# Gate columns and the last 120 mz columns in one block of weights, in a fused attention and mLSTM kernel

## The reference, cut to what matters

```
h = rms_norm(x, pre_norm_g)
proj = h @ w_in          # 1024 x 4616: aq ak av az mq mk mv mo mz (512 columns each), mi (4), mf (4)
ya = moba_attention(rope(aq), rope(ak), av);  ya = rms_norm(ya) * silu(az)
q, k = silu(causal_conv(mq | mk))
hm = mlstm(q, k, mv, mi + i_bias, mf + f_bias)      # 4 heads of 128
ym = sigmoid(mo) * groupnorm(hm) * silu(mz)
out = x + rms_norm((ya | ym) @ w_out) * post_g
```

## Time and profile before

| | us |
|---|---|
| median of 3 runs (lowest, highest) | 319.71 (317.78, 320.05) |
| the profiled execution's own time | 318.38 |
| its span, first to last instruction | 316.6 |
| PE busy | 308.4 (97%) |
| DVE busy | 225.9 (71%) |
| ACT busy | 164.9 (52%) |
| POOL busy | 96.7 (31%) |

### The profile page before, as it was taken

How to read it: one execution, slowest core, us unless ns; L and a number is a source line. 1 busy time by engine, 2 the same in 40 slices (tenths; PEclk the granted TensorE clock), 3 DMA queues, 4 the chain that set the end, 5 groups by cost and what they waited for, 6 DMA issues and landing times.

```text
span 316.6 us, 4991 instructions
## 1 busy us (share of the span) xinstructions
PE 308.4 (97%) x1595; PEld 255.7 (81%) x1595; DVE 225.9 (71%) x509; ACT 164.9 (52%) x337; POOL 96.7 (31%) x121
## 2 busy tenths in 40 slices
PE   7999999999999999999999999999999999999992
PEld 4888888878888888888888888778888888888882
DVE  3544999748998699968998568965577766856534
ACT  3448856287345324573147573385556976453201
POOL 3701006066450114002220026592711984000000
PEclk9999999999999999999999999999999999999998
DMA  7941553956725486654865433211220474310111
GB/s 233 313 99 36 158 144 94 164 154 155 142 69 135 135 151 204 182 144 114 181 193 183 114 77 88 71 66 34 67 68 0 127 185 157 134 68 0 66 68 67
DMA packets 29177, 38.30 MB, mean 121 GB/s; under 512 B 3672, under 2 KB 15296, under 8 KB 29152
## 3 DMA queue, kind: packets, MB, share of 16 engines
q1 hardware_dynamic: 27424, 34.51, 36.7%
q0 software_dynamic: 1568, 3.34, 7.3%
q10 hardware_dynamic: 160, 0.14, 0.1%
HBM read 33.68 MB, written 4.29 MB: 120 GB/s over the span
## 4 chain that ended last, share of the span: by engine, by line
PE 82%; DVE 7%; issue 4%; DMA 3%; ACT 2%; DVEq 0%; POOLq 0%; POOL 0%; SPq 0%; ACTq 0%
PE bank L1501 21%; PE bank L1503 21%; PE bank L1502 20%; PE bank L1553 4%; PE bank L1849 3%; PE bank L1793 3%; DMA w_raw<-in_w_in 3%; PE bank L1814 3%; PE bank L1646 2%; DVE w_lo L1061 2%; DVE farena L1173 1%; PE bank L1743 1%; PE bank L1534 1%; PE bank L1804 1%; PE bank L1647 1%
## 5 line engine op out<-in xcount | busy, mean ns | idle before, releaser
L788 ACT ACTIVATE w_hi<-w_raw 128x512 fp32r<-128x512 f32 x71 | 43.7, 626 | 63.1 <-PE bank L1503 50.8
L1501 PE MATMUL bank<-w_hi,xT_hi 128*128 128x512 f32 (+1 forms) x180 | 72.5, 403 | 0.0
L1503 PE MATMUL bank<-w_hi,xT_lo 128*128 128x512 f32 (+1 forms) x180 | 69.7, 387 | 0.0
L1502 PE MATMUL bank<-w_lo,xT_hi 128*128 128x512 f32 (+1 forms) x180 | 69.4, 385 | 0.0
L1061 DVE TENSOR_TENSOR w_lo<-w_raw,w_hi 128x512 fp32r<-128x512 f32 x64 | 45.6, 724 | 10.3 <-ACT w_hi L788 10.2
L1501 PE MATMUL bank<-xT_hi,w_hi 128*128 128x512 f32 x128 | 50.8, 397 | 0.0
L1503 PE MATMUL bank<-xT_hi,w_lo 128*128 128x512 f32 x128 | 50.1, 392 | 0.0
L1502 PE MATMUL bank<-xT_lo,w_hi 128*128 128x512 f32 x128 | 50.0, 390 | 0.0
L1503 PEld LDWEIGHTS bank<-w_hi,xT_lo 128*128 128x128 f32 x180 | 33.8, 188 | 7.1
L1501 PEld LDWEIGHTS bank<-w_hi,xT_hi 128*128 128x128 f32 x180 | 33.9, 188 | 5.9 <-issue 0.4
L1502 PEld LDWEIGHTS bank<-w_lo,xT_hi 128*128 128x128 f32 x180 | 34.0, 189 | 5.5
(11 more groups left out here) (215 smaller groups left out, 583.4 us busy)
## 6 DMA issues: line engine op xcount, KB each, us to landing
w_raw<-in_w_in SPq DMA_DIRECT2D x72, 256.0 KB, 3.0
w_raw<-in_w_out SPq DMA_DIRECT2D x16, 256.0 KB, 2.9
kq_rows<-stage SPq DMA_DIRECT2D x8, 256.0 KB
gy<-kq_rows SPq DMA_DIRECT2D x8, 256.0 KB, 3.5
gy<-in_x SPq DMA_DIRECT2D x4, 512.0 KB, 5.9
out_y<-gy SPq DMA_DIRECT2D x7, 256.0 KB, 2.0
farena<-in_x SPq DMA_DIRECT2D x4, 256.0 KB, 4.3
farena<-in_x SPq DMA_DIRECT2D x2, 512.0 KB, 6.3
```

The costliest lines, as they stand in the source:

```text
L788: a.activation(hi, raw, ACT.Copy).then_inc(w_hi_done, 1)
L1501: pe.matmul(o, hi, m_hi, start=start, stop=False)
L1502: pe.matmul(o, hi, m_lo, start=False, stop=False)
L1503: return pe.matmul(o, lo, m_hi, start=False, stop=stop)
```

## The change

The 8 gate columns and the last 120 columns of mz (`MIX_W`) make one block of 128 weight columns, loaded like the mq and mk blocks in two "heads" slots, 7 and 8, ahead of mv's last slot (now 9). `mix_slot` multiplies it with the weights stationary: 24 matmuls of 512 columns into bank 7, rows 0 to 119 mz, 120 to 127 gates. `gate_rows_of`, `wg`, its DMA, its clearing and its four DVE instructions go. DVE scales bank 7 (`scaled_rows`), and two stream shuffles repeat the gate rows; ACT copies the unscaled block into `mix_rows`. The mz slots (now 58 to 65) take 392 columns (`MZ_W`), and four transposes (`mz_mixed`) put the 120 columns behind them into each bank. `mix_rows` is the tile of `causal`, so POOL builds the mask later, behind the first mz slot. All slot numbers from mq on are higher by 2. On ACT the first sum of squares moves ahead of cut 6, the mix copy, Abs and Exp come ahead of `mv_high`, and the i gate's bias stays behind it; two more cuts come ahead of it, and so on DVE ahead of `mv_low`.

```diff
+MIX_W = P - 8
+MZ_W = AW - MIX_W
+MIX = MG - MIX_W
+SLOTS = [("in", "cols", k, MVC) for k in range(NK - 1)]
+SLOTS += [("in", "heads", k, MIX) for k in (0, 4)] + [("in", "cols", NK - 1, MVC)]
+def width(n):
+    return MZ_W if S_MZ <= n < S_MZ + NK else AW
...
-            g.memset(wg[:].bitcast(F32), 0.0).then_inc(wg_clear, 1)
-            g.memset(causal[:], 0.0).then_inc(cleared, 1)
...
+            g.wait_ge(w_used, S_MZ + 1)
+            g.memset(causal[:], 0.0).then_inc(cleared, 1)
+            g.wait_ge(cleared, 5)
+            g.affine_select(out=causal[:, SEQ - P:], in_=causal[:, SEQ - P:], compare_op=ALU.is_ge, fill=FAR, base=0,
+                            pattern=[[-1, P]], channel_multiplier=1).then_inc(causal_done, 1)
...
-                if k >= 6:
-                    x_squares(k - 6)
-            x_squares(2)
-            x_squares(3)
-            for n in range(RING, RING + 4):
+                if k >= 5:
+                    x_squares(k - 5)
+            cut(RING)
+            x_squares(NT - 1)
+            for n in range(RING + 1, RING + 6):
                 cut(n)
-            a.wait_ge(gate_ps, 1)
-            a.wait_ge(gate_clear, 1)
-            a.activation(gate_low_rows, bank[7][P // 2:, :], ACT.Copy).then_inc(gate_split, 1)
+            a.wait_ge(scaled, 1)
+            a.activation(mix_rows[:], bank[7][:], ACT.Copy).then_inc(mix_done, 1)
+            a.wait_ge(gate_sb, 1)
+            a.activation(rows[0], f_rows[96:112, :], ACT.Abs, bias=bcol[:, 1:2]).then_inc(absf_done, 1)
+            a.wait_ge(absf_done, 1)
+            a.activation(rows[1], rows[0], ACT.Exp, scale=-1.0).then_inc(expf_done, 1)
             for t in range(NT):
                 mv_high(t)
...
-            link(v.tensor_tensor(gate_rows, bank[7][0:P // 2, :], gate_low_rows, ALU.add))
-            v.tensor_tensor(gate_rows, gate_rows, rbc[0:P // 2, :], ALU.mult).then_inc(gate_sb, 1)
             cut(RING + 2)
-            cut(RING + 3)
+            v.wait_ge(w_used, S_MIX + 2)
+            v.tensor_tensor(scaled_rows, bank[7][:], rbc[:], ALU.mult).then_inc(scaled, 1)
+            v.wait_ge(scaled, 1)
+            v.stream_shuffle(f_rows, scaled_rows, [28 + i % MH for i in range(32)]).then_inc(gate_sb, 1)
+            v.stream_shuffle(i_rows, scaled_rows, [24 + i % MH for i in range(32)]).then_inc(gate_sb, 1)
+            for n in range(RING + 3, RING + 6):
+                cut(n)
             for t in range(NT):
                 mv_low(t)
...
+            def mix_slot(c):
+                low_done(pe, S_MIX + c)
+                pe.wait_ge(xt_lo, x_parts(4 * c + 3))
+                for kk in range(4):
+                    k = 4 * c + kk
+                    mm = product(bank[7][:], *w_part(S_MIX + c, slice(kk * P, (kk + 1) * P)), xT_hi[:, k, :],
+                                 xT_lo[:, k, :], k == 0, k == NK - 1)
+                mm.then_inc(w_used, 1)
...
-            gate_rows_of()
+            mix_slot(0)
             rx_rows()
+            mix_slot(1)
             mv_slot(NK - 1)
...
+            def mz_mixed(t):
+                pe.wait_ge(v_raw, t + 1)
+                pe.transpose(bank[t][:, MZ_W:], mix_rows[0:MIX_W, t * P:(t + 1) * P], ident[0:MIX_W, 0:MIX_W])
```

More of the change, by code:

```diff
@@ L318, in build @@
         rows = [gy[0:16, i // 4, i % 4, :] for i in range(8)]
-        gate_rows, gate_low_rows = (stage[0:P // 2, i, :] for i in range(2))
+        gate_rows = stage[0:P // 2, 0, :]
+        mix_rows = causal
+        scaled_rows, i_rows, f_rows = (stage[:, i, :] for i in range(1, NT))
         bcol = pcol[0:16, R_BIAS:R_END]
@@ L550, in _ @@
                 if kind == "cols":
-                    src = w[0, k * P:(k + 1) * P, c:c + AW]
-                    dst = w_raw[:, n % RAW, :]
+                    src = w[0, k * P:(k + 1) * P, c:c + width(n)]
+                    dst = w_raw[:, n % RAW, 0:width(n)]
                 else:
@@ L614, in _ @@
             g.memset(upad[:, :, 0:KCONV - 1], 0.0).then_inc(cleared, 1)
-            g.wait_ge(cleared, 5)
+            g.wait_ge(cleared, 4)
             g.memset(mhalf[:], -0.5).then_inc(consts, 1)
             g.wait_ge(ident_done, 1)
-            g.affine_select(out=causal[:, SEQ - P:], in_=causal[:, SEQ - P:], compare_op=ALU.is_ge, fill=FAR, base=0,
-                            pattern=[[-1, P]], channel_multiplier=1).then_inc(consts, 1)
             g.affine_select(out=causalT[:], in_=causalT[:], compare_op=ALU.is_ge, fill=FAR, base=0,
@@ L784, in cut @@
                     a.wait_ge(w_used, n - RING + 1)
-                hi, raw = w_hi[:, n % RING, :], w_raw[:, n % RAW, :]
+                hi, raw = w_hi[:, n % RING, 0:width(n)], w_raw[:, n % RAW, 0:width(n)]
                 if by_blocks(n):
@@ L824, in _ @@
                 x_hi(k)
-                if k >= 6:
-                    x_squares(k - 6)
-            x_squares(2)
-            x_squares(3)
-            for n in range(RING, RING + 4):
-                cut(n)
-            a.wait_ge(gate_ps, 1)
-            a.wait_ge(gate_clear, 1)
-            a.activation(gate_low_rows, bank[7][P // 2:, :], ACT.Copy).then_inc(gate_split, 1)
+                if k >= 5:
[3 more added lines that the diff above has]
+            for n in range(RING + 1, RING + 6):
+                cut(n)
+            a.wait_ge(scaled, 1)
[4 more added lines that the diff above has]
+            a.activation(rows[1], rows[0], ACT.Exp, scale=-1.0).then_inc(expf_done, 1)
             for t in range(NT):
                 mv_high(t)
[L837 to L841, removed]
+            a.wait_ge(gate_sb, 2)
+            a.activation(rows[6], i_rows[96:112, :], ACT.Identity, bias=bcol[:, 0:1]).then_inc(igate_done, 1)
             def decays(h, j):
@@ L1057, in cut @@
                 v.wait_ge(w_hi_done, n + 1)
-                lo, raw, hi = w_lo[:, n % RING, :], w_raw[:, n % RAW, :], f32(w_hi[:, n % RING, :])
+                cols = slice(0, width(n))
+                lo, raw, hi = w_lo[:, n % RING, cols], w_raw[:, n % RAW, cols], f32(w_hi[:, n % RING, cols])
                 if by_blocks(n):
@@ L1128, in gate_low @@
                 v.wait_ge(gate_sb, 1)
-                link(v.tensor_scalar(rows[3], gate_rows[32:48, :], bcol[:, 1:2], 0.0, ALU.add, ALU.min))
+                link(v.tensor_scalar(rows[3], f_rows[96:112, :], bcol[:, 1:2], 0.0, ALU.add, ALU.min))
                 v.wait_ge(expf_done, 1)
@@ L1373, in mask @@
                     v.wait_ge(prob_done, s - 1)
+                if s == 0:
+                    v.wait_ge(causal_done, 1)
                 at = score_at(s)
@@ L1542, in by_slot @@
                         free(t)
-                    mm = product(bank[t][:], *part(k, t), *w_part(n), k == 0, k == nk - 1)
+                    mm = product(bank[t][:, 0:width(n)], *part(k, t), *w_part(n, slice(0, width(n))), k == 0,
+                                 k == nk - 1)
                     if k == nk - 1 and t < NT - 1:
```

39 lines of the change are left out of this document (16 added, 23 removed).

## The result

The changed kernel is slightly slower: median 321.5 us (19 runs) against 318.13 us for the kernel before (19 runs, the first three among them). Its four longest runs (323.4 to 323.6 us) count as slow and are left out of the ratio, which compares the means of the others, 320.74 us, and of the kernel before, 318.53 us: 1.0069, 95% interval 1.0043 to 1.0095, which is +2.2 us (+1.4 to +3.0). By the medians it is +3.4 us. The forecast was 320.6 us within 317.1 to 323.0, +0.8 us.

The account below looks back on a forecast made before the run. PE's unbroken stream was taken as the bound, other engines hidden only while they stay ahead. +1.7 (mix for gate products) +0.7 (gate chain) -1.6 (kept of mz) = +0.8 us on median 319.71: 320.5, stated as 320.6, range 317.1 to 323.0.

Parts of the forecast that it names:

- PE's own sum: PE's matmuls: +1.7 us for mix slots replacing gate products, -4.5 for narrow mz slots, +0.4 for transposes: -2.4 us.
- The first half as a whole: Mix path in place of the gate products, up to `weighted`: +1.7 us on PE and +0.7 from the later gate work.
- The waits of the start: PE's `rx_rows` waiting for POOL's `rx`: `rx` comes about 0.6 us earlier, at 30.8, so costed at nothing.
- The gate chain: DVE's run from mix slot 1 through `gate_low` to the first decay masks: without room, so PE loses +0.7 us.
- The mz stage: PE needs 4.1 us less up to `z_part(0, 0)` but waits for DVE's `mz_gate`, keeping only 1.6 us.
- the shift is carried to the end: Behind `z_part(0, 0)` PE is again behind DVE by more than a microsecond, so the shift there stays.
- The first, PE bounds the mz stage: Rival: DVE's run shortens with PE, the whole 4.1 us is kept, gate chain without loss: 317.3 us, chance 0.2.
- The second, a gate chain 3 us late: Rival: gate work misses its slot loads, 3 us late instead of 0.7 at the first decay masks: 322.9 us, chance 0.15.
- The third, 392 columns at the price of 512: Rival: mz matmuls of 392 columns still step by 0.227 us, so mz gives +0.4: 322.5 us, chance 0.05.

Follow-up runs that it names:

- the control: The kernel before with the same three waits that hold back POOL's cuts of mo slots, nothing else changed: ratio 1.0000, median 317.96 us.

## Why the prediction was right, and what it missed

**PE's own sum** held. `rx_rows` began at 31.20, forecast 31.26. The narrow matmuls step by 0.177 us (taken: 0.180), and the four transposes add 0.47 us (taken: 0.44). The first half as a whole: +2.4 us forecast, +2.5 between the profiled executions at `weighted`, +2.4 by the ratio of the kernel with full mz slots.

**The waits of the start** cost nothing, as costed: `rx` was done at 30.5 us (forecast 30.8, before 31.36), ahead of `rx_rows` at 31.20. The earlier sum of squares is the reason given; no kernel was run without it.

**The gate chain.** `gate_low` was forecast for 43.4 us and came at 43.12; the wait for `weighted` for 1.4 us and was 1.5. That the wait follows the start of `gate_low` is likely, not shown. The two kernels with the chain shorter on ACT have waits of 0.8 and 0.6 us, less than any other with the mix path. But in those others `gate_low` starts 11.9 us behind `rx_rows` every time, and the wait is anything from 0.9 to 1.5 us. So the 1.5 us of the profile agree with the forecast of 1.4 in part by luck. The reason, too, was half wrong. The step said that DVE carries the chain; up to `gate_low` ACT does, by its mix copy, Abs, Exp, `mv_high` and the i gate, and two DVE cuts taken out of the way changed nothing. The prediction's own times had ACT at 41.0 us ahead of DVE's last three cuts; only its reading of them named DVE.

**The mz stage** went as written: narrow slots, an unshortened run on DVE (15.6 us forecast, 15.8 measured), two waits of 2.9 us in sum in step 2 (2.5 forecast). Of the 4.1 us the profiled execution kept 2.5 - 1.2 = 1.3 us at `z_part(0, 0)` (1.6 forecast). The two kernels with POOL held back show the cause by taking it away, the control shows that it isn't the waits, and the narrow slots on the kernel before show it without the mix path. The rule of the Trainium skill ("SBUF — State Buffer", "Who interferes with whom") was the lead to it. The 128x2 instruction went from 1.17 to 0.16 us once POOL's cut was out of its way, which agrees with the rule.

**What was missing is the clock.** The forecast for `z_part(0, 0)` was +0.8 us and 1.2 were measured; the prediction then had "the shift is carried to the end". It isn't: 1.5 us more were lost at the lower clock level right behind the gaps. The step that failed is that a wait was priced by its own length. In the four executions of the changed kernel with a clock of 0.994 or more, the time was 318.1 to 319.7 us, 319.0 in the mean, where the forecast of +0.8 on top of 318.13 gives 318.9; in the 15 others 320.0 to 323.6. The profiled execution (0.991) is a mild one of these: 13 have 0.986 or 0.987 and a median of 321.8 us. None of them was profiled. The narrow slots alone were, at 0.986, and there the lower level lasted some 6 us, not 3.5.

**Luck in the number.** The 320.6 us were built on 319.71, the median of three runs of the kernel before; its median over 19 runs is 318.13. On that the same sum gives 318.9, and 321.5 were measured. The high start hid most of what the sum left out. The change itself was forecast at +0.8 us and measured at +2.2 by the ratio, and 0.8 lies under its interval of 1.4 to 3.0.

**The rivals.** The first, PE bounds the mz stage, is ruled out by the narrow slots alone. The second, a gate chain 3 us late, didn't come. The third, 392 columns at the price of 512, is refuted by the step of 0.177.

Not settled: why the clock fell behind the gaps in most executions and not in all; how much of the wait at 73 us hangs on the slot loads beside the decay rows, as no kernel was run that moves those loads; and what it would take to end the last 0.8 us at `mz_gate`.

## What to carry to other kernels

Where one engine is busy in an unbroken stream, work taken off it is worth only what its suppliers are ahead: find the next product that waits, take its spare time (here 0.8 us), and trace back which run of another engine sets it. Before taking work off TensorE late in a stage, free that run: here three waits on POOL, worthless in the kernel before, were the condition for most of the gain. And price a new gap in TensorE's stream with what the clock does behind it, or fill it.

## What the runs showed of the hardware that was not expected

Gaps of 1.8 and 1.1 us, with 0.9 us of matmuls and 0.66 of transposes between them, were enough for the granted clock to fall. In the profile of the changed kernel it fell behind the second; in two others, the narrow slots alone and the shorter chain on ACT, it had fallen before the second began, so there the first was enough. The fall shows in 15 of 19 executions of the changed kernel and in 8 of 12 with narrow slots alone (mean clock 0.991 or less), in none of 12 with the gaps filled and none of 12 with POOL held back, where a gap of 0.8 us was left. In the profile of the kernel before, the matmuls behind its one gap of 0.7 us at 70 us keep their step; of its 80 executions in the three series one has 0.989, the others 0.994 or more.

The start has two lengths as well, in kernels with the same code there. In the profiled execution of the kernel before with POOL held back, the second four matmuls take 1.91 us:

```profile
7.39 1.91 PE L1559 MATMUL bank<-w_hi,xT_lo 128*128 128x512 f32 x4
```

In the kernel before the same four take 1.08 us. The profile's clock reads 1.00 there in both, so the mean clock of an execution doesn't show this. `rx_rows` then starts at 33.77 us instead of 32.26: 1.5 us that have nothing to do with the edit, and a likely cause of the spread of 317 to 320 us that the kernel before has; that was not tried.
